# A two-layer diffusion backbone in one kernel: hand-overs at norms, first mixer projections and down products, and decay matrices built by accumulated products

## The chip, the cores and the metric

The kernel runs on one core of one Trainium2 chip. The metric is the device time of one execution in microseconds (us); lower is better. Each kernel is run several times and the median is given.

## What is computed

384 tokens (128 of context, 256 of latent, with weights in common) go through two layers of width 1024. Each layer is a SwiGLU feed-forward, a token mixer and a second feed-forward, each followed by a residual sum and a layer norm:

```python
def _layernorm(x, g, b):
    mu = mean(x); var = mean((x - mu)**2)
    return (x - mu) * rsqrt(var + LN_EPS) * g + b

def _layer(x, mod, p, states):      # sh, sc, g: nine parts of mod
    x = _layernorm(ALPHA * x + 0.5 * g1 * _swiglu(x * (1 + sc1) + sh1, w_gu[0], w_down[0]), ...)
    y, new_states = _token_mixer(x * (1 + sc2) + sh2, p, states)
    x = _layernorm(ALPHA * x + g2 * y, ...)
    x = _layernorm(ALPHA * x + 0.5 * g3 * _swiglu(x * (1 + sc3) + sh3, w_gu[1], w_down[1]), ...)
```

The mixer projects its input once (`w_in`) into the operands of three branches that run over the tokens forward and backward: HGRN2 (a gated linear recurrence), mLSTM (four heads with a matrix memory) and SSD (eight heads). The branches are projected, gated, summed and projected again (`w_out`). For mLSTM and SSD each head and direction needs a matrix of decays between tokens t and s of one block, which is masked to one triangle before the exponential:

```python
dlog = where(causal, b[t] - b[s] + i[s], -inf)          # mLSTM
s    = exp(dlog - m[t]) * (q @ k.T)
seg  = where(causal, a[t] - a[s], -inf)                 # SSD
y    = (exp(seg) * (C @ B.T)) @ (x * dt)
```

All is float32 in and out; the feed-forwards have 2816 hidden columns.

## The kernel before

**Layout and products.** Features lie on partitions in `KC` = 8 chunks of 128, the `T` = 384 tokens are columns. The weights are streamed once, in units of 512 KB (128 rows of 1024 columns), by SyncE's queue into four buffers `raw`. ScalarE rounds each unit to the fp32r type (`whi`, round_unit, L974), GpSimd subtracts to get the rest (`wlo`, L519, two halves a unit). TensorE then makes three products for each chunk instead of one in full fp32: high weight with high input, high with low input, low with high input (block_product, L552 to L554). Inputs are split in the same way: ScalarE shifts and scales a chunk (shifted, L1022, two pieces a chunk: context and latent tokens apart), rounds it to `h_hi` (rounded, L1028), and VectorE subtracts to `h_lo` (low, L1460). At the head of each projection three blocks are interleaved chunk by chunk (leading_products, L566 to L568), since the input's chunks come one after the other.

**What sets the order.** There is no scheduler: each engine's program is written out by hand, and counting semaphores order the engines. Some stages are separated by a meeting of TensorE, ScalarE and VectorE:

```python
def meet(eng, n):
    eng.drain().then_inc(met, 1)
    eng.wait_ge(met, 3 * n)
```

**The stages of a layer** and where they lie in layer 0 of the profiled execution: first feed-forward, gate and up products (122 to 307 us), its down products (309 to 404.7), norm (to 417.2), input projections (to 507), HGRN2 (to 654), rows of decays (to 741), mLSTM (to 797), convolution and states, SSD (939.5 to 1048), branches, output projection (to 1171.3), norm (to 1184.9), second feed-forward (to 1467.5), norm (to 1479.6). Layer 1 follows in the same way and ends with a norm that has no product behind it.

**Norms.** residual (VectorE, L1479) adds a block's output to `x`, one block of 128 features after the other. statistics (VectorE, L1482 on) subtracts an old mean, adds chunks 0 to 6 up in `sx` and their squares (ScalarE, squares, L1030) in `sqs` (L1512). layer_norm on TensorE (L595 to L604) makes four fp32 products with a matrix of 1/1024, two for the mean into bank 5 and two for the squares into bank 6: the sum of chunks 0 to 6, and chunk 7 by itself (L602 for the mean's second one). layer_norm on VectorE (L1515 on) then subtracts the mean from each chunk (L1527), forms the variance (L1533), takes the reciprocal of ScalarE's root (L1045; L1538), multiplies each chunk (L1543), and between those makes the low parts of the next input. Four subtractions stand ahead of the reciprocal.

**Banks of the input projections.** The plan (mixer_order, and L402 on) gives each projected block a bank of PSUM. `hf`, `hi` and `hg` are outputs of the input projection for HGRN2; `hf` comes first:

```python
kind, banks = "tm", (2, 3, 4) if name == "hi" else (5, 6, 7)
pool = {"rows": (3, 4), "ml": (3, 3), "pairs": (3, 7)}.get(stage, (0, 1))
banks = (b if name == "hf" and b < LEAD else pool[k % 2],)
```

So three leading blocks use banks 0 to 2, and the fourth bank 1 again, which ScalarE must have read out before (project_out and the bodies at L1303).

**Feed-forward.** Gate and up blocks go to banks 0 to 3; VectorE multiplies them (`vb`, L1563), copies to `act_hi` and subtracts to `act_lo`. Behind them all three engines go through ffn_met (L461): a meeting, and in the first feed-forward of layer 1 a reset of all counters instead. Then the down products start in banks 0 and 1.

**Decay matrices.** rows (VectorE, L1721 on) leaves in `x_5` one row of 384 numbers for each head and direction. For each of 8 rounds of mLSTM and 16 of SSD in a layer: spread (TensorE, L773) puts one row on all partitions by a fp32 product with a column of the identity, broadcast; exps (VectorE, L1808) adds the mask `neg` (-1e30 outside of the triangle) into `pt`; pair (ScalarE, L1217) takes the exponential with a per-row bias, three pieces of 128 columns; scores (VectorE, L1818 and L1823) multiplies with the products of q and k; TensorE's next products take that (L787 second product of a round, L805 heads, L810 to L812 and `carry`, L1837 on, for the carried state `cs`; L880 in SSD). L780 makes q with k. Between the rounds stand other projections of the same layer, by mixer_order.

## Time and profile before

| what | us |
|---|---|
| median of 3 runs (lowest to highest) | 2798.45 (2794.81 to 2804.83) |
| profiled execution: time / span in the trace | 2796.18 / 2794.3 |
| TensorE matmul, busy | 2431.0 |
| GpSimd, busy | 1518.8 |
| VectorE, busy | 1196.1 |
| ScalarE, busy | 1061.3 |
| ScalarE's rounding of a unit (L974), mean of one | 1.036 |
| GpSimd's rest of half a unit (L519), mean of one | 1.335 |
| VectorE's wait for ScalarE ahead of lastw (L1793, in rows), layer 0 and 1 | 11.58 and 10.37 |
| VectorE's wait for TensorE at the start (L1430) | 2.98 |

A line of the trace's timeline gives start and length in us, engine, line, operation, output and inputs by the program's names (without their buffer numbers), the shape, the count of like instructions in a row, and in brackets how long the engine had waited and for which instruction. A source view gives the number of instructions, the shortest, median and longest in ns, and the first and last start. The granted clock is given as a share: 1.00 is 2.4 GHz, 0.50 is 1.2 GHz.

### The profile page before, as it was taken

To read this page: it belongs to the slowest core of one execution; us is meant where nothing else is said; L and a number is where in the kernel's file an instruction comes from. 1 tells how busy PE (TensorE), PEld (TensorE's weight loads), DVE (VectorE), ACT (ScalarE), POOL (GpSimd) and SP (SyncE) were. 2 spreads that over 40 slices of the span, in tenths; PEclk is the share of its full clock that TensorE was granted. 3 is DMA by queue.
4 is the path that set the end of the run, shared out by engine and by line. 5 is a ranking of instruction groups with operands and counts; after the bars stand their busy time and mean duration, and the time that the engine had idled before them with its cause. 6 is when DMAs were issued, how large, how long until landed. Compare 5 with 4: busy or idle time off the path is not lost. (4 is left out here: it accounts for less than half of the span.)

```text
span 2794.3 us, 38271 instructions
## 1 busy us (share of the span) xinstructions
PE 2431.0 (87%) x13246; PEld 2222.2 (80%) x13246; DVE 1196.1 (43%) x1923; ACT 1061.3 (38%) x1631; POOL 1518.8 (54%) x1164
## 2 busy tenths in 40 slices
PE   5599989898878887799998999889987787889997
PEld 2499989787646676699998999788775676889997
DVE  4543232562565326643225331526445543663314
ACT  4333235434444443343234322452444324143322
POOL 3376545565555774466664655456743432646653
PEclk8799999999989998999999999999998888899999
DMA  8443333344343552234343333333432221324432
GB/s 277 144 141 122 118 108 109 103 129 129 102 128 94 159 158 83 83 120 123 118 128 100 124 112 118 97 113 121 144 105 83 85 66 61 98 76 135 128 111 70
DMA packets 93459, 323.16 MB, mean 116 GB/s; under 512 B 11040, under 2 KB 14368, under 8 KB 92960
## 3 DMA queue, kind: packets, MB, share of 16 engines
q1 hardware_dynamic: 87552, 312.03, 35.8%
q10 hardware_dynamic: 5792, 9.56, 1.0%
q8 instruction: 76, 1.25, 0.2%
q14 instruction: 39, 0.32, 0.0%
HBM read 317.35 MB, written 4.20 MB: 115 GB/s over the span
## 5 line engine op out<-in xcount | busy, mean ns | idle before, releaser
L519 POOL TENSOR_TENSOR wlo<-raw,whi 128x512 fp32r<-128x512 f32 (+2 forms) x1160 | 1518.6, 1335 | 1243.2 <-ACT whi L974 1182.0
L974 ACT CAST whi<-raw 128x1024 fp32r<-128x1024 f32 (+1 forms) x600 | 615.8, 1036 | 998.8 <-PE ps L554 666.4
L552 PE MATMUL ps<-h_hi,whi 128*128 128x384 f32 x2224 | 762.9, 343 | 35.2 <-DVE h_lo L2025 13.0
L554 PE MATMUL ps<-h_hi,wlo 128*128 128x384 f32 x2224 | 752.8, 339 | 0.0
L553 PE MATMUL ps<-h_lo,whi 128*128 128x384 f32 x2224 | 752.7, 338 | 0.0
L552 PEld LDWEIGHTS ps<-h_hi,whi 128*128 128x128 f32 x2224 | 425.5, 191 | 45.6 <-DVE h_lo L2025 13.6
L553 PEld LDWEIGHTS ps<-h_lo,whi 128*128 128x128 f32 x2224 | 425.4, 191 | 2.6 <-issue 2.0
L554 PEld LDWEIGHTS ps<-h_hi,wlo 128*128 128x128 f32 x2224 | 424.6, 191 | 0.0
L552 PE MATMUL ps<-act_hi,whi 128*128 128x384 f32 x704 | 241.9, 344 | 11.5 <-DVEq L458 5.9
L553 PE MATMUL ps<-act_lo,whi 128*128 128x384 f32 x704 | 240.4, 341 | 0.0
L554 PE MATMUL ps<-act_hi,wlo 128*128 128x384 f32 x704 | 240.3, 341 | 0.0
L1479 DVE SCALAR_TENSOR_TENSOR x<-ps,mod,x 128x128 f32<-128x128 f32 x96 | 35.6, 412 | 349.5 <-PE ps L554 349.5
L1560 DVE SCALAR_TENSOR_TENSOR sb<-tb,ps 128x384 f32<-128x384 f32 x88 | 48.8, 554 | 245.2 <-ACT tb L1061 245.2
L578 PE MATMUL ps<-whi,cond_s 128*4 128x512 f32 x288 | 123.7, 430 | 34.5 <-POOL wlo L519 34.5
L552 PEld LDWEIGHTS ps<-act_hi,whi 128*128 128x128 f32 x704 | 133.7, 190 | 13.3 <-DVEq L458 6.9
L1569 DVE TENSOR_TENSOR act_lo<-vb,act_hi 128x384 f32 x88 | 131.2, 1490 | 10.8
L553 PEld LDWEIGHTS ps<-act_lo,whi 128*128 128x128 f32 x704 | 133.5, 190 | 0.5
L554 PEld LDWEIGHTS ps<-act_hi,wlo 128*128 128x128 f32 x704 | 133.6, 190 | 0.0
L1563 DVE SCALAR_TENSOR_TENSOR vb<-sb,ps 128x384 f32<-128x384 f32 x88 | 48.8, 554 | 180.2 <-PE ps L554 180.0
L578 PE MATMUL ps<-wlo,cond_s 128*4 128x512 f32 x288 | 121.2, 421 | 0.0
L686 PE MATMUL ps<-q,kk 128*128 128x128 f32 x768 | 98.3, 288 | 22.8 <-DVEq L458 14.0
L686 PEld LDWEIGHTS ps<-q,kk 128*128 128x128 f32 x768 | 95.0, 202 | 28.0 <-DVEq L458 14.8
(311 smaller groups left out, 3011.7 us busy)
## 6 DMA issues: line engine op xcount, KB each, us to landing
raw<-in_w_in SPq DMA_DIRECT2D x248, 512.0 KB, 3.5
raw<-in_w_gu SPq DMA_DIRECT2D x176, 512.0 KB, 3.4
raw<-in_w_down SPq DMA_DIRECT2D x64, 512.0 KB, 3.4
raw<-in_w_mod SPq DMA_DIRECT2D x40, 512.0 KB, 4.5
raw<-in_w_down SPq DMA_DIRECT2D x32, 384.0 KB, 3.0
raw<-in_w_branch SPq DMA_DIRECT2D x24, 512.0 KB, 3.4
raw<-in_w_out SPq DMA_DIRECT2D x16, 512.0 KB, 3.4
x<-in_x ACTq DMA_DIRECT2D x1, 1536.0 KB, 6.9
```

Of the source, the lines that this page charges most:

```text
L519: last = nc.gpsimd.tensor_tensor(wlo[s][:, a:b], raw[s][:, a:b], whi[s][:, a:b].bitcast(F32), ALU.subtract)
L552: mm(out, hi_, xh[:, xc, :], start=start and n == 0, stop=False)
L553: mm(out, hi_, xl[:, xc, :], start=False, stop=False)
L554: last = mm(out, lo_, xh[:, xc, :], start=False, stop=stop and n == len(chunks) - 1)
L578: last = mm(bank[0:4, :], cond_s[:, 2 * m + c, :], w[s][:, c * MIX:(c + 1) * MIX], start=(m == 0 and c == 0 and w is whi), stop=(m == 3 an ...
L686: last = mm(out, kk[:, d, g, cols], (q if what == "diag" else qd[d])[:, g, cols], start=True, stop=True)
L974: act.copy(whi[m][:, 0:w], raw[m][:, 0:w]).then_inc(w_hi, 1)
L1479: last = stt(x[:, b, a:c], ps[b % 2][:, a:c], mod[:, col, gi:gi + 1], x[:, b, a:c], ALU.mult, ALU.add)
L1560: step(stt(sbf[jj][:, :], tb[jj][:, :], 1.0, ps[2 * jj][:, 0:T], ALU.add, ALU.mult))
L1563: stt(vb[jj][:, :], sbf[jj][:, :], 0.5, ps[2 * jj + 1][:, 0:T], ALU.mult, ALU.mult).then_inc(gated, 1)
L1569: step(tt(act_lo[:, bass.ds(f, 1), :], vb[jj][:, :].unsqueeze(1), act_hi[:, bass.ds(f, 1), :].bitcast(F32), ALU.subtract))
```

## The change

The change rewrites four kinds of places and touches what they share:

- *Norms.* Chunk 6 is no longer added to the sums: `sx` and `sqs` hold chunks 0 to 5 (`SUMMED` = 6), and chunks 6 and 7 each get a product of their own for mean and squares, six products instead of four. On VectorE two subtractions instead of four stand ahead of the reciprocal, and the low part of chunk n comes two steps behind its multiplication instead of three. On ScalarE chunk 0 is shifted and rounded before chunk 1 is shifted.
- *First mixer projections.* The blocks of that stage take banks 0 to 4 in turn; `hi` moves to banks 5 to 7 and `hg` to 2 to 4. ScalarE loads the tanh table ahead of the stage by a one-column activation.
- *Down products.* The meeting between gate and down products goes. TensorE waits for the count of gated chunks, and, within the first down block, for a new count of low parts (`ff_lo`), third by third. VectorE waits for that count, one step back, ahead of the product that overwrites `vb`. The reset of the counters in layer 1's first feed-forward stays (counts_reset).
- *Decay matrices.* spread makes three fp32r products accumulated in one bank: the identity with the mask, repeated for the three blocks of columns, and the broadcast column with the high and the low part of the rows (`x_5h`, `x_5l`, which rows splits on VectorE). VectorE's mask addition (exps) is gone, and the exponential reads PSUM. Identity and mask are rounded to fp32r once, at the start.

```diff
-        ident = sb("ident", [P, P])
+        ident_r = sb("ident_r", [P, P], F32R)
+        ident = ident_r[:, :].bitcast(F32)
...
-        neg = sb("neg", [P, 2, P])
+        neg = sb("neg", [P, 2, P], F32R)
...
+        (x_5h, x_5l, pr0, pr1, st0, st1), e3 = region(
+            rows0, ("x_5h", [P, T], F32R), ("x_5l", [P, T], F32R), *[(n, [P, T]) for n in ("pr0", "pr1", "st0", "st1")])
...
-        SHIFT_N = 3
+        SHIFT_N, SUMMED = 3, KC - 2
...
-                    kind, banks = "tm", (2, 3, 4) if name == "hi" else (5, 6, 7)
+                    kind, banks = "tm", (2, 3, 4) if name == "hg" else (5, 6, 7)
                 else:
                     kind = name if name in ("mod", "turn") else "fm"
-                    pool = {"rows": (3, 4), "ml": (3, 3), "pairs": (3, 7)}.get(stage, (0, 1))
-                    banks = (b if name == "hf" and b < LEAD else pool[k % 2],)
+                    pool = {"in": (0, 1, 2, 3, 4), "rows": (3, 4), "ml": (3, 3), "pairs": (3, 7)}.get(stage, (0, 1))
+                    banks = (pool[k % len(pool)],)
...
-        def ffn_met(eng, l, j, owner):
+        def counts_reset(eng, l, j, owner):
 
             if l == 0 or j == 1:
-                meet(eng, MEET["ffn", j])
...
-                pe.wait_ge(ln_y, j + 1)
-                mm(ps[5][:, 0:T], mean_w[:, :], sx[:, :], start=True, stop=False)
-                pe.wait_ge(ln_q, (KC - 1) * (j + 1))
-                mm(ps[6][:, 0:T], mean_w[:, :], sqs[:, :], start=True, stop=False)
-                pe.wait_ge(ln_cent, KC * (j + 1))
-                mm(ps[5][:, 0:T], mean_w[:, :], x[:, KC - 1, :], start=False, stop=True).then_inc(ln_mean, 1)
-                pe.wait_ge(ln_sq, KC * (j + 1))
-                mm(ps[6][:, 0:T], mean_w[:, :], sq[(KC - 1) % 4][:, :], start=False, stop=True).then_inc(ln_acc, 1)
+                for n in range(-1, 2):
+                    if n < 0:
+                        pe.wait_ge(ln_y, j + 1)
+                    else:
+                        pe.wait_ge(ln_cent, KC * j + KC - 1 + n)
+                    last = mm(ps[5][:, 0:T], mean_w[:, :], sx[:, :] if n < 0 else x[:, KC - 2 + n, :], start=(n < 0),
+                              stop=(n == 1))
+                    if n == 1:
+                        last.then_inc(ln_mean, 1)
+                    if n < 0:
+                        pe.wait_ge(ln_q, SUMMED * (j + 1))
+                    else:
+                        pe.wait_ge(ln_sq, KC * j + KC - 1 + n)
+                    last = mm(ps[6][:, 0:T], mean_w[:, :], sqs[:, :] if n < 0 else sq[(KC - 2 + n) % 4][:, :],
+                              start=(n < 0), stop=(n == 1))
+                last.then_inc(ln_acc, 1)
...
-                ffn_met(pe, l, j, "pe")
+                counts_reset(pe, l, j, "pe")
+                if l and not j:
+                    at = 0
+                pe.wait_ge(gated, at + NF + 2)
                 for b in range(KC):
                     pe.wait_ge(resid, 2 * KC * j + b + 1)
                     for third in range(KTHIRDS):
                         u = u0 + U_GU + KTHIRDS * b + third
                         unit_split(pe, l, u)
+                        if b == 0:
+                            pe.wait_ge(ff_lo, at + 2 + min(KC * (third + 1), NF))
...
-            def spread(r, rr):
-
+            def spread(r, d, rr):
+
+                out = ps[r % 2][:, 0:T]
                 if r >= 2:
-                    pe.wait_ge(pr_x, r - 1)
-                mm(ps[r % 2][:, 0:T], ident[:, rr:rr + 1].to_broadcast([P, P]), x_5[:, :], start=True,
-                   stop=True).then_inc(pr_bc, 1)
+                    pe.wait_ge(pr_e, r - 1)
+                mm(out.rearrange("p (a b) -> p a b", b=P), ident_r[:, :], neg[:, d:d + 1, :].to_broadcast([P, NT, P]),
+                   start=True, stop=False)
+                row = ident_r[:, rr:rr + 1].to_broadcast([P, P])
+                mm(out, row, x_5h[:, :], start=False, stop=False)
+                mm(out, row, x_5l[:, :], start=False, stop=True).then_inc(pr_bc, 1)
...
-                for n in range(KC + 1):
+                shifted(j + 1, 0)
+                rounded(j + 1, 0)
+                for n in range(1, KC + 1):
                     if n < KC:
                         shifted(j + 1, n)
-                    if n:
+                    if n > 1:
...
-                act.wait_ge(pr_x, r + 1)
+                act.wait_ge(pr_bc, r + 1)
...
-                    last = af(pr[r % 2][:, c], pt[r % 2][:, c], ACT.Exp, bias=t_1[:, t, rr:rr + 1])
+                    last = af(pr[r % 2][:, c], ps[r % 2][:, c], ACT.Exp, bias=t_1[:, t, rr:rr + 1])
...
+                af(eps[:, 2:3], eps[:, 0:1], ACT.Tanh)
...
+            cp(ident_r[:, :], ident_in[:, :])
+            cp(neg[:, :, :], neg_in[:, :, :])
...
-                    if n == 0:
+                    if n in (0, KC - 2):
                         continue
                     dve.wait_ge(ln_cent, KC * j + n + 1)
                     step.done()
                     sum_ = tt(sx[:, :], x[:, 0, :] if n == 1 else sx[:, :], x[:, n, :], ALU.add)
-                    sum_.then_inc(ln_y, 1) if n == KC - 2 else step(sum_)
-                for n in {4: (1,), 5: (2, 3), 6: (4, 5, 6)}.get(b, ()):
+                    sum_.then_inc(ln_y, 1) if n == KC - 3 else step(sum_)
+                for n in {4: (1,), 5: (2, 3), 6: (4, 5)}.get(b, ()):
...
-                shift(2)
-                shift(3)
                 dve.wait_ge(ln_std, j + 1)
                 step(nc.vector.reciprocal(rstd[:, :], std[:, :]))
                 step.done()
-                for n in range(KC + 3):
+
+                def normalised(n):
+
+                    dve.wait_ge(ln_sub, KC * j + n + 1)
+                    tt(x[:, n, :], x[:, n, :], rstd[:, :], ALU.mult).then_inc(ln_out, 1)
+
+                normalised(0)
+                normalised(1)
+                for n in range(2, KC + 2):
                     if n < KC:
-                        dve.wait_ge(ln_sub, KC * j + n + 1)
-                        tt(x[:, n, :], x[:, n, :], rstd[:, :], ALU.mult).then_inc(ln_out, 1)
-                    if n + 4 < KC:
-                        shift(n + 4)
-                    if not final and n >= 3:
-                        low(j + 1, n - 3)
+                        shift(n)
+                        normalised(n)
+                    if not final:
+                        low(j + 1, n - 2)
...
+                        dve.wait_ge(ff_lo, i * 2 + (at + jj + 1))
...
-                        step(tt(act_lo[:, bass.ds(f, 1), :], vb[jj][:, :].unsqueeze(1),
-                                act_hi[:, bass.ds(f, 1), :].bitcast(F32), ALU.subtract))
-                assert step.n - n0 == 6
-                step.off, step.n = 0, n0 + 6 * (U_GU // 4)
-                ffn_met(dve, l, j, "dve")
+                        tt(act_lo[:, bass.ds(f, 1), :], vb[jj][:, :].unsqueeze(1),
+                           act_hi[:, bass.ds(f, 1), :].bitcast(F32), ALU.subtract).then_inc(ff_lo, 1)
...
+                step(cp(x_5h[:, :], x_5[:, :]))
+                step.done()
+                step(tt(x_5l[:, :], x_5[:, :], x_5h[:, :].bitcast(F32), ALU.subtract))
...
-            def exps(r, d):
-                dve.wait_ge(pr_bc, r + 1)
-                if r >= 2:
-                    dve.wait_ge(pr_e, r - 1)
-                tt(pt[r % 2][:, :].rearrange("p (a b) -> p a b", b=P),
-                   neg[:, d:d + 1, :].to_broadcast([P, NT, P]),
-                   ps[r % 2][:, 0:T].rearrange("p (a b) -> p a b", b=P), ALU.add).then_inc(pr_x, 1)
```

VectorE at the end of the first norm (L1527 subtracts the mean, L1533 is the variance, L1543 multiplies, L1460 is the first low part), before:

```order
L1527 TENSOR_TENSOR x<-x,ps 128x384 [waits ln_dsq,ln_sq,ln_mean,dve_step]
L1533 TENSOR_TENSOR rstd<-ps,std 128x384 [waits ln_acc]
L1527 TENSOR_TENSOR x<-x,ps 128x384 [waits ln_sq] x3
L1538 RECIPROCAL rstd<-std 128x384 [waits ln_std]
L1543 TENSOR_TENSOR x<-x,rstd 128x384 [waits ln_sub,dve_step]
L1527 TENSOR_TENSOR x<-x,ps 128x384 [waits ln_sq]
L1543 TENSOR_TENSOR x<-x,rstd 128x384 [waits ln_sub]
L1527 TENSOR_TENSOR x<-x,ps 128x384 [waits ln_sq]
L1543 TENSOR_TENSOR x<-x,rstd 128x384 [waits ln_sub]
L1527 TENSOR_TENSOR x<-x,ps 128x384 [waits ln_sq]
L1543 TENSOR_TENSOR x<-x,rstd 128x384 [waits ln_sub]
L1527 TENSOR_TENSOR x<-x,ps 128x384 [waits ln_sq]
L1460 TENSOR_TENSOR h_lo<-ht_99,h_hi 128x384 [waits md_hi]
```

and of the change (L1550, L1556, L1559, L1565 and L1483 are the same operations in that order):

```order
L1550 TENSOR_TENSOR x<-x,ps 128x384 [waits ln_dsq,ln_sq,ln_mean,dve_step]
L1556 TENSOR_TENSOR rstd<-ps,std 128x384 [waits ln_acc]
L1550 TENSOR_TENSOR x<-x,ps 128x384 [waits ln_sq]
L1559 RECIPROCAL rstd<-std 128x384 [waits ln_std]
L1565 TENSOR_TENSOR x<-x,rstd 128x384 [waits ln_sub,dve_step]
L1565 TENSOR_TENSOR x<-x,rstd 128x384 [waits ln_sub]
L1550 TENSOR_TENSOR x<-x,ps 128x384 [waits ln_sq]
L1565 TENSOR_TENSOR x<-x,rstd 128x384 [waits ln_sub]
L1483 TENSOR_TENSOR h_lo<-ht_99,h_hi 128x384 [waits md_hi]
```

One subtraction instead of three now stands between variance and reciprocal, and three operations instead of seven between the first multiplication and the first low part.

TensorE from the last leading block to the fourth block of the input projections (the numbers are those of banks and tiles; `whi` and `wlo` are the weight's parts), before:

```order
L566 MATMUL ps2<-h_hi_62,whi2_55 128x384
L567 MATMUL ps2<-h_lo_63,whi2_55 128x384
L568 MATMUL ps2<-h_hi_62,wlo2_59 128x384
L552 MATMUL ps1<-h_hi_62,whi3_56 128x384 [waits w_split,evac]
L553 MATMUL ps1<-h_lo_63,whi3_56 128x384
L554 MATMUL ps1<-h_hi_62,wlo3_60 128x384
```

and of the change:

```order
L567 MATMUL ps2<-h_hi_62,whi2_55 128x384
L568 MATMUL ps2<-h_lo_63,whi2_55 128x384
L569 MATMUL ps2<-h_hi_62,wlo2_59 128x384
L553 MATMUL ps3<-h_hi_62,whi3_56 128x384 [waits w_split]
L554 MATMUL ps3<-h_lo_63,whi3_56 128x384
L555 MATMUL ps3<-h_hi_62,wlo3_60 128x384
```

The fourth block moved from bank 1 to bank 3, and its wait for the emptied bank (`evac`) is gone; the wait for the weights stays.

TensorE in the second round of mLSTM of layer 0 (`x_5` holds the rows, `ident` the identity, `cs` the carried state, `st` the scores; L585 is a projection's turn that stands between), before:

```order
L812 MATMUL ps7<-cs_162,mq_107 128x129
L585 MATMUL ps3<-pick_75,modrow_180 128x2 [waits evac]
L585 MATMUL ps3<-pick_75,modrow_180 128x2 x3
L773 MATMUL ps1<-x_5_135,ident_64 128x384 [waits pr_x]
L787 MATMUL ps7<-cs_162,mq_107 128x129 [waits ml_cu]
L805 MATMUL ps4<-va_109,st0_155 128x129 [waits ml_h,pr_s]
L805 MATMUL ps4<-va_109,st0_155 128x129 x2
L810 MATMUL ps6<-va_109,kw0_183 128x129 [waits ml_kw]
```

and of the change:

```order
L830 MATMUL ps7<-cs_164,mq_109 128x129
L586 MATMUL ps3<-pick_75,modrow_182 128x2 [waits evac]
L586 MATMUL ps3<-pick_75,modrow_182 128x2 x3
L788 MATMUL ps1<-neg_66,ident_r_64 128x384 [waits pr_e]
L791 MATMUL ps1<-x_5h_153,ident_r_64 128x384
L792 MATMUL ps1<-x_5l_154,ident_r_64 128x384
L805 MATMUL ps7<-cs_164,mq_109 128x129 [waits ml_cu]
L823 MATMUL ps4<-va_111,st0_157 128x129 [waits ml_h,pr_s]
L823 MATMUL ps4<-va_111,st0_157 128x129 x2
L828 MATMUL ps6<-va_111,kw0_185 128x129 [waits ml_kw]
```

Three products stand in the place of one, and they wait for ScalarE's exponential of two rounds before (`pr_e`) instead of VectorE's mask addition (`pr_x`).

## Rows read from the trace of the kernel before

**Rows 1.** The page, part 1: busy us, share of the span, instructions of each engine.

```profile
PE 2431.0 (87%) x13246; PEld 2222.2 (80%) x13246; DVE 1196.1 (43%) x1923; ACT 1061.3 (38%) x1631; POOL 1518.8 (54%) x1164
```

**Rows 2.** Stretches: window, us, busy PE, PEld, DVE, ACT, POOL, clock, DMA, GB/s.

```profile
140.00:210.00 70.00, 70.00 (x406) 70.00 (x405) 28.90 (x37) 21.02 (x25) 49.32 (x38) 1.00 0.45 143
310.45:313.80 3.35, 3.35 (x12) 3.35 (x12) 0.00 (x0) 0.00 (x0) 2.29 (x2) 0.50 0.00 0
...
1373.00:1376.50 3.50, 3.49 (x20) 3.49 (x21) 0.00 (x0) 1.04 (x1) 2.38 (x2) 1.00 0.01 5
```

**Rows 3.** Timeline of VectorE, end of the first norm.

```profile
408.83 1.47 DVE L1527 TENSOR_TENSOR x<-x,ps 128x384 f32<-128x384 f32 x3
410.22 2.54 DVE L1538 RECIPROCAL rstd<-std 128x384 f32<-128x384 f32 x1
412.80 0.56 DVE L1543 TENSOR_TENSOR x<-x,rstd 128x384 f32<-128x384 f32 x1
```

**Rows 4.** Timeline of TensorE, first norm and the first product behind it.

```profile
404.66 0.81 PE L598 MATMUL ps<-sx,mean_w 128*128 128x384 f32 x2
405.30 0.81 PE L600 MATMUL ps<-sqs,mean_w 128*128 128x384 f32 x2
406.25 0.91 PE L602 MATMUL ps<-x,mean_w 128*128 128x384 f32 x2
...
417.23 0.66 PE L566 MATMUL ps<-h_hi,whi 128*128 128x384 f32 x1 [9.42 <-DVE h_lo L1460]
```

**Rows 5.** Timeline of ScalarE, first norm: root, shifted chunks, rounding.

```profile
408.94 0.61 ACT L1045 ACTIVATE std<-rstd,eps 128x384 f32<-128x384 f32 x1 [1.26 <-DVE rstd L1533]
413.39 1.92 ACT L1022 ACTIVATE ht<-x,lnab 128x128 f32<-128x128 f32 x4 [3.83 <-DVE x L1543]
415.21 0.50 ACT L1028 CAST h_hi<-ht 128x384 fp32r<-128x384 f32 x1
```

**Rows 6.** Timeline, norm behind the output projection: VectorE, then TensorE.

```profile
1169.87 2.75 DVE L1512 TENSOR_TENSOR sqs<-sqs,sq 128x384 f32<-128x384 f32 x3
1172.54 0.73 DVE L1479 SCALAR_TENSOR_TENSOR x<-ps,mod,x 128x128 f32<-128x128 f32 x2
...
1177.89 2.54 DVE L1538 RECIPROCAL rstd<-std 128x384 f32<-128x384 f32 x1
...
1171.14 0.81 PE L598 MATMUL ps<-sx,mean_w 128*128 128x384 f32 x2
...
1173.92 0.91 PE L602 MATMUL ps<-x,mean_w 128*128 128x384 f32 x2 [0.33 <-DVE x L1497]
```

**Rows 7.** Timeline behind the leading blocks: ScalarE's table load, TensorE's fourth block.

```profile
432.14 1.28 ACT L1303 ACT_TABLE_LOAD   x1
...
435.69 0.44 PE L552 MATMUL ps<-h_hi,whi 128*128 128x384 f32 x1 [3.03 <-ACT kk L1303]
```

**Rows 8.** Timeline from the last gated chunk to the first down product.

```profile
307.26 0.55 DVE L1563 SCALAR_TENSOR_TENSOR vb<-sb,ps 128x384 f32<-128x384 f32 x1 [2.38 <-PE ps L554]
...
309.11 0.45 PE L552 MATMUL ps<-act_hi,whi 128*128 128x384 f32 x1 [1.98 <-DVEq L458]
```

**Rows 9.** Source views: mask addition, exponential from SBUF, an activation from PSUM.

```profile
L1808 DVE TENSOR_TENSOR pt<-neg,ps x48: 542/554/555, 742.0 to 2348.7; 128x384 f32<-128x384 f32 x48
...
L1217 ACT ACTIVATE pr<-pt,t x144: 384/387/405, 742.6 to 2349.9; 128x128 f32<-128x128 f32 x144
...
L1107 ACT ACTIVATE y_hg<-ps,par x24: 359/368/378, 683.7 to 2051.4; 128x128 f32<-128x128 f32 x24
```

**Rows 10.** Who waited for VectorE's carry and scores (us, times): mLSTM, last SSD.

```profile
  PE ps L787: 12.2, 11
...
  PE ps L805: 4.9, 8
  PE ps L780: 4.0, 6
...
  PE ps L880: 5.4, 5
```

**Rows 11.** Timeline of TensorE, an SSD round of layer 0 with its fourth unit.

```profile
971.72 0.40 PE L578 MATMUL ps<-whi,cond_s 128*4 128x512 f32 x1 [1.79 <-POOL wlo L519]
```

More of the change, by code:

```diff
@@ L788, in second @@
                        stop=True).then_inc(ml_i2, 1)
-                spread(0, 0)
+                spread(0, 0, 0)
                 head(0)
@@ L795, in mlstm @@
                     if r < 7:
-                        spread(r + 1, 32 * (1 - d) + (r + 1) // 2)
+                        spread(r + 1, 1 - d, 32 * (1 - d) + (r + 1) // 2)
                     if r:
@@ L868, in group @@
                     last.then_inc(pr_qk, 1)
-                spread(8, 64)
+                spread(8, 0, 64)
                 group(0)
@@ L1556, in ffn @@
                 with dve.Fori(0, U_GU // 4) as i:
-                    step.off = i * 6
+                    step.off = i * 4
                     for jj in range(2):
@@ L1791, in rows @@
                 dve.wait_ge(row_d, 3)
+                step.done()
+                step(cp(x_5h[:, :], x_5[:, :]))
+                step.done()
+                step(tt(x_5l[:, :], x_5[:, :], x_5h[:, :].bitcast(F32), ALU.subtract))
                 dve.wait_ge(row_a, 5)
@@ L2029, in _ @@
             for _ in range(2):
+                dve.sem_inc(ff_lo, 1)
                 dve.sem_inc(gated, 1)
```

56 lines of the change are left out of this document (26 added, 30 removed).

## The prediction, on record before the change was run

> **What bounds the kernel now.** I read the page's busy times first: TensorE is busy for 2431.0 of 2794.3 us [rows 1], so the time is its work plus its gaps, and an edit on another engine counts only where TensorE waits for it. Then the table by stretches [rows 2]: in a dense stretch 406 products of 128x384 take 70.00 us, 0.172 us each, at the granted clock 1.00 (2.4 GHz); behind some gaps the clock is 0.50 (1.2 GHz) and 12 products take 3.35 us, where after an equal gap with the clock kept 20 take 3.50 us. So a gap that is followed by such a stretch costs about 1.5 us more than its own length. Then I read the timelines at the four places that the diff touches, for what ends TensorE's wait there. The sum is made against the profiled execution, 2796.2 us (span 2794.3 and 1.9 around it); the median of the runs is 2.3 above that.
>
> **Norms.** TensorE stops with the last down product and starts again when the first low part of the next input is there: from 404.66 to 417.23 at the first norm [rows 4].
>
> *Later:* of chunks 6 and 7 now both go to the sums as products of their own. Before, two products (0.64 us apart, 404.66 and 405.30) stood ahead of the one that ends the mean, which started at 406.25. Now four stand there: 404.66 + 4 x 0.64 = 407.22, so mean, variance and root come 0.97 us later.
>
> *Earlier:* the reciprocal started at 410.22 [rows 3], though the root was ready at 408.94 + 0.61 = 409.55 [rows 5], because three subtractions (408.83, 1.47 us) stood ahead of it on VectorE. Now one does. It starts at 409.55 + 0.97 + 0.1 = 410.6, only 0.4 late.
>
> *Earlier again:* from the first multiplication (412.80 [rows 3]) to TensorE's start were 4.43 us, because ScalarE shifted two chunks (413.39, four pieces in 1.92 us) before it rounded the first (415.21 [rows 5]), and VectorE had seven operations between that multiplication and the first low part. Now: 0.59 to ScalarE's start, 0.96 for the two pieces of chunk 0, 0.50 rounding, 0.55 low part (VectorE, with three operations between, is there by then), 0.1 of hops: 2.7. That is 1.7 earlier; the net is 1.3 per norm, at three norms (the first of each layer, and the last of layer 0): -3.9. The later chunks come every 1.6 us (three VectorE operations each); TensorE needs 9 x 0.172 = 1.55 for one at full clock and twice that at its cold start, so it hardly waits for them.
>
> *The two norms behind the output projection* gain more. There VectorE is late: three additions of squares (1169.87, 2.75 us) keep the last residual until 1172.54, although TensorE ended at 1171.3 [rows 6]. With two additions it starts about 1171.5. The last mean product then starts at 1171.14 + 4 x 0.64 = 1173.7 instead of 1173.92, so the root is 0.2 earlier, and the reciprocal, freed of two subtractions, at 1177.1 instead of 1177.89: 0.8, plus the 1.7 of the hand-over: 2.5 each, -5.0.
>
> *The last norm* has no product behind it. It gets the 0.4, and two subtractions (0.47 each) now stand behind the reciprocal: +1.4. **Norms together -7.5**; bounds -2 (only the hand-over, at two norms) and -12 (no delay of the mean at all).
>
> **First mixer projections.** After the three leading blocks the fourth waited 3.03 us for ScalarE to empty bank 1, with a table load of 1.28 us in between [rows 7]. It now goes to bank 3 and the fifth to bank 4, both free: no wait. The next cover is the weights: the fifth block's unit can be rounded once the leading blocks end, about 1 us of emptying, 1.0 of rounding and 2 x 1.34 on GpSimd (the table of the profile) = 4.7 us after; TensorE has the rest of the leading blocks and 24 x 0.172, some 5.1 us, of work until then. So 3.0 goes, and the cold stretch that followed it in both layers, 1.5: 2 x 4.5, **-9.0**; bounds -5 and -9.5. The loading of the tanh table hides in ScalarE's idle time there. Ahead of the cover there is nothing else: the stage's end moves with TensorE.
>
> **Down products.** The last gated chunk ends at 307.26 + 0.55 = 307.8; TensorE starts at 309.11, after act_hi, act_lo and a meeting of three engines [rows 8]. Now it waits for the last gated chunk (banks 0 and 1 are read by then) and for the low parts of the first eight chunks only, long there: 307.9, 1.2 earlier. The low part of the last chunk is needed some 8 us later. This holds in three of four feed-forwards; in the third the counters are still reset in a meeting. In two of the three the gap was followed by a cold stretch [rows 2]; behind a gap of 0.8 us I take the clock as kept: -3 x 1.2 - 2 x 1.5, **-6.6**; bounds -3 and -6.6. The added wait on VectorE ahead of the gated product is for a subtraction one step back, done long before.
>
> **Decay matrices.** 48 times, a fp32 product (two passes) put a row on all partitions, VectorE added the mask (0.554 us, L1808), ScalarE took the exponential [rows 9]. Now three accumulated products do both. Their duration is not in the trace as such; the nearest row is the dense stretch, whose products have the same type, shape and a new weight block each: 3 x 0.172 = 0.52, against 0.64 for the two passes of a fp32 product (404.66 to 405.30 [rows 4]). Taken: 0.52. Upper bound: 0.45 each, half of the pair of passes at 406.25 that ran alone, 0.91 [rows 4]; 1.36 together. ScalarE's exponential reads PSUM instead of SBUF: 0.368 against 0.387 us on rows of 128 columns [rows 9], taken as no change.
>
> The Trainium skill, "VectorE: DVE Perf Modes", section on the TRN2 errata, gives ScalarE 172 fixed cycles from PSUM and 224 from SBUF, so by it three pieces would save 0.13 us a pair, an estimate of 2 to 3 us over the pairs on the path. The rows here show 0.02 a piece, so the sum stays without it.
>
> *mLSTM rounds* (16 in two layers): TensorE waits there for VectorE, 12.2 us for the carried state, 4.9 + 4.0 for the scores [rows 10]. The mask addition stood on VectorE ahead of the scores, and the exponential ahead of ScalarE's weighing of the second product, which the heads and the carried state wait for. Lower bound: one VectorE slot of 0.47 per round, 7.5. Upper bound: all those waits, 21, and 16 x 0.12 for the products. I take 10.5, because heads and carried state are late next on VectorE: what goes from the scores' waits comes back in part as a wait for the carried state. *SSD rounds* (32): 0.12 us each, 3.8. Where a round has no projection to fill it, the wait for scores of 5.4 in five places [rows 10] shrinks by the mask addition and its hops, 0.7: three such rounds and the two first ones, 3.5. In layer 0, four rounds wait 1.79 us for GpSimd's fourth unit [rows 11]; its rounding stands on ScalarE behind the exponential, which now starts 0.65 earlier: 2.6. **Decay together -20.4**; bounds -8 and -32.
>
> The two operations that split the rows (1 us, by L1808's size) fall into VectorE's wait of over 10 us for ScalarE in that stage; rounding identity and mask at the start falls into its wait of 3 us for TensorE (both waits in the table of the profile). Both at nothing; without that cover they would cost 2 x 1 us and 0.5 us.
>
> **Sum.** -7.5 - 9.0 - 6.6 - 20.4 = -43.5: 2752.7 for an execution like the profiled one, 2755.0 at the median's height. Forecast: **2754**.
>
> **Rivals.**
> 1. *The clock stretches come back elsewhere.* Gaps of 0.8 us remain at the down products, and one of three gaps of 2 us was not followed by a cold stretch, so length alone does not settle it. Without the 6 us of clock: 2760.
> 2. *GpSimd takes over.* It is busy for 54% of the span [rows 1] and makes TensorE wait in layer 0's SSD rounds already. If its splitting paces those rounds and the mLSTM rounds of layer 0, half the decay gain goes: 2764.
> 3. *The clock gains more.* Cold stretches lie in the mLSTM and SSD rounds too; six fewer at 1.5 are 9 us: 2745.
> 4. *The three products do not overlap.* At the upper bound of 0.45 us each, a row costs 0.71 more than now, 34 us, and the 5.7 I counted as saved go: 2795, no change.
> 5. *The other side, slower:* each product takes a whole isolated fp32 pair, 0.65 us, since one weight block is a single column spread out and the moving block a repeated mask. Then 48 x (1.95 - 0.65) = 62 stand against the other 43.5 - 5.7 = 37.8: 24.6 over the median, 2823. It decides from 0.48 us a product on, where 48 x (1.44 - 0.65) = 38 eats them. Against it: the fp32 row product used the same spread column, at no visible price.
>
> **How the numbers follow.** Chances: forecast 0.52, rival 1 0.13, rival 2 0.12, rival 3 0.16, rival 4 0.04, rival 5 0.03. The bounds of the terms move the forecast by some 15 up and down; the range 2738 to 2776 takes in rivals 1 to 3 and leaves out 4, 5 and the far ends of the bounds. 0.3% of 2798 is 8.4 us, about what a measurement can tell here. Faster by more: 0.93 (forecast, rivals 1 to 3); within: 0.04 (rival 4); slower: 0.03 (rival 5).
>
> **What would show it.** In the new trace: TensorE's gap at the first norm shorter by about 1.3 us with the reciprocal right behind the root; no gap behind the leading blocks; the down gap 0.8 us; three spread products within 0.55 us; no wait for a mask addition, a longer share of waits on the carried state. Wrong would be the forecast if a spread takes over 1 us, if GpSimd's waits grow by 10 us, or if cold stretches stand behind the shortened gaps.

## The result, and the profile after

The changed kernel takes **2762.37 us** (median of 4 runs, 2761.27 to 2765.39), beside 2796.63 for the kernel before on the same chip: a ratio of 0.9879, 95% interval 0.9862 to 0.9896. It is faster by 34.3 us. The forecast was 2754, a gain of some 43; the range of 2738 to 2776 holds the time.

The page's first part of the changed kernel; [rows 1] are those of before:

```profile
PE 2421.6 (88%) x13318; PEld 2228.6 (81%) x13318; DVE 1186.8 (43%) x1869; ACT 1057.6 (38%) x1633; POOL 1522.0 (55%) x1164
```

Busy times say little here: TensorE's fell by 9.4 us, the span by 33.9 (2794.3 to 2760.4). So most of the gain lies in gaps, and to find it I took the start of the first product of each stage from both timelines. The distance from one such start to the next, in us, both profiled executions:

| stage (layer 0 / layer 1) | before | after | difference | forecast |
|---|---|---|---|---|
| norms behind down products, a product follows (3) | 12.57, 12.58, 12.57 | 11.27, 11.27, 11.27 | -3.9 | -3.9 |
| norms behind the output projection (2) | 13.76, 13.75 | 11.27, 11.27 | -5.0 | -5.0 |
| last norm, to the end | 20.32 | 22.29 | +2.0 | +1.4 |
| input projections | 97.41 / 96.82 | 92.45 / 92.52 | -9.3 | -9.0 |
| gate and up, three feed-forwards | 187.19, 188.11 / 186.83 | 186.51, 186.58 / 186.34 | -2.7 | -3.6 |
| down products behind those | 95.55, 94.02 / 95.55 | 94.02, 94.02 / 94.02 | -3.1 | -3.0 |
| **gate and up, layer 1's first** | 192.77 | 198.29 | **+5.5** | 0 |
| mLSTM | 81.31 / 70.88 | 79.18 / 66.22 | -6.8 | -10.5 |
| SSD | 116.66 / 89.79 | 112.57 / 84.99 | -8.9 | -9.9 |
| HGRN2 | 219.54 / 215.85 | 215.73 / 219.16 | -0.5 | 0 |

What is left out comes to -1.3. Two lines differ from the forecast by clearly more than a microsecond: layer 1's first feed-forward, and mLSTM (SSD differs by 1.0).

The first norm in the new trace, TensorE, VectorE and ScalarE (lines as in [rows 3 to 5], shifted in the new file):

```profile
402.44 0.81 PE L603 MATMUL ps<-sx,mean_w 128*128 128x384 f32 x2
...
405.02 0.81 PE L603 MATMUL ps<-x,mean_w 128*128 128x384 f32 x2
...
413.71 0.66 PE L567 MATMUL ps<-h_hi,whi 128*128 128x384 f32 x1 [7.23 <-DVE h_lo L1483]
...
407.50 0.54 DVE L1550 TENSOR_TENSOR x<-x,ps 128x384 f32<-128x384 f32 x1
408.26 2.55 DVE L1559 RECIPROCAL rstd<-std 128x384 f32<-128x384 f32 x1 [0.22 <-ACT std L1063]
...
413.00 0.56 DVE L1483 TENSOR_TENSOR h_lo<-ht,h_hi 128x384 fp32r<-128x384 f32 x1
...
411.44 0.98 ACT L1040 ACTIVATE ht<-x,lnab 128x128 f32<-128x128 f32 x2 [3.21 <-DVE x L1565]
412.46 0.51 ACT L1046 CAST h_hi<-ht 128x384 fp32r<-128x384 f32 x1
```

The mean's last product starts 2.58 us behind the first (1.59 before), and now VectorE waits for ScalarE's root ahead of the reciprocal (0.22), where it was late before. The low part starts 4.74 us behind the reciprocal's start (408.26 to 413.00); before, TensorE got its first one 7.01 behind it (410.22 to 417.23), now 5.45.

The fourth block of the first input projections and the first down product; [rows 7 and 8] are those of before:

```profile
428.77 0.44 PE L553 MATMUL ps<-h_hi,whi 128*128 128x384 f32 x1 [0.69 <-POOL wlo L520]
...
308.42 0.44 PE L553 MATMUL ps<-act_hi,whi 128*128 128x384 f32 x1 [0.80 <-DVE vb L1591]
```

Gaps of 0.69 and 0.80 us are left of 3.03 and 1.98, and no cold stretch (products at the granted clock of about 0.5) follows. The 0.80 is what the forecast named; the 0.69, for GpSimd's part of the weights, was not foreseen at this block. In layer 1 the fourth block has no gap: its leading blocks end 15.25 us behind the stage's first product, those of layer 0 14.37.

The decay matrices, source views of the changed kernel (count, ns as shortest/median/longest, first and last start; the last line is of those that waited for the carried state):

```profile
L788 PE MATMUL ps<-neg,ident_r x48: 331/338/687, 729.4 to 2317.8; 128*128 128x384 f32 x48
L791 PE MATMUL ps<-x_5h,ident_r x48: 332/338/522, 729.7 to 2318.0; 128*128 128x384 f32 x48
L1237 ACT ACTIVATE pr<-ps,t x144: 342/368/370, 730.3 to 2319.1; 128x128 f32<-128x128 f32 x144
  PE ps L805: 20.1, 9
```

A product is shown with 338 ns, but the next one starts 0.17 us behind it in a dense stretch. One round of SSD in layer 0, TensorE:

```profile
964.52 0.34 PE L788 MATMUL ps<-neg,ident_r 128*128 128x384 f32 x1
964.69 0.34 PE L791 MATMUL ps<-x_5h,ident_r 128*128 128x384 f32 x1
964.87 0.33 PE L792 MATMUL ps<-x_5l,ident_r 128*128 128x384 f32 x1
```

The next product starts at 965.04, so the three take 0.52 us. The exponential takes 368 ns from PSUM, 387 from SBUF [rows 9]: 0.019 us a piece. The Trainium skill, "VectorE: DVE Perf Modes", section on the TRN2 errata, has 52 cycles between the two; the measured difference is less than half of the 0.043 a piece that the prediction's estimate took from it, and decides. TensorE's waits for the scores (4.9 and 4.0 [rows 10]) are gone, but the wait for the carried state is 20.1 us where it was 12.2 [rows 10].

### The profile page after: what moved, and what is told of

It is laid out like the page before. It is cut to its first block, busy times and chain, and to the rows that moved or that the text cites. A ratio compares the mean times of both kernels' runs of the same rounds, so it can differ in the third digit from the quotient of the medians.

```text
span 2760.4 us, 38398 instructions
## 1 busy us (share of the span) xinstructions
PE 2421.6 (88%) x13318; PEld 2228.6 (81%) x13318; DVE 1186.8 (43%) x1869; ACT 1057.6 (38%) x1633; POOL 1522.0 (55%) x1164
## 4 chain that ended last, share of the span: by engine, by line
issue 46%; POOL 42%; PE 10%; DVE 1%; POOLq 1%; ACT 0%; DVEq 0%; ACTq 0%
POOL wlo L520 42%; PE ps L553 3%; PE ps L555 3%; PE ps L554 3%; POOLq L534 0%; POOLq L532 0%; DVE ht L1476 0%; DVE x L1565 0%; DVE x L1550 0%; ACT whi L992 0%; DVE h_lo L1483 0%; DVE x L1577 0%; DVE rstd L1559 0%; PE ps L603 0%; PE ps L611 0%
## 5 line engine op out<-in xcount | busy, mean ns | idle before, releaser
L520 POOL TENSOR_TENSOR wlo<-raw,whi 128x512 fp32r<-128x512 f32 (+2 forms) x1160 | 1521.8, 1337 | 1204.1 <-ACT whi L992 1142.3
```

The costliest lines, as they stand in the source:

```text
L520: last = nc.gpsimd.tensor_tensor(wlo[s][:, a:b], raw[s][:, a:b], whi[s][:, a:b].bitcast(F32), ALU.subtract)
```

## The experiments

Twelve kernels, each run several times beside the kernel before. The changes are against the changed kernel unless the text says otherwise; "..." marks code left out. They were run in four sets, in which the kernel before had medians of 2793.4 to 2797.4 us. Only e2, e5, e6 and e12 have an interval of the ratio that stands clear of the changed kernel's (0.9862 to 0.9896); for the others the stages of the traces carry the reading, and the difference of the medians does not by itself. The stretch ahead of the first gate product, which no edit here touches, took 119.9 to 124.7 us in these traces.

**e1, an earlier wait at the layer boundary.** Layer 1's first feed-forward lost 5.5 us. Before it, ScalarE waits for VectorE's last affine operation of the norm, loads parameters, and only then rounds the weights of the fourth block.

```diff
-                    act.wait_ge(ln_x, KC * 4)
+                    act.wait_ge(ln_out, KC * 3)
```

> The changed kernel with one wait moved: at the layer boundary ScalarE waits for the last multiplication of the norm (24 counts of ln_out) instead of VectorE's last affine operation (32 counts of ln_x) before it loads the next parameters and rounds weights. Theory 1 (the hand-over of the norms made TensorE come early for a weight unit that ScalarE rounds only behind that wait, 4.48 us in layer 1's first feed-forward where 1.29 were before, with a cold stretch behind it): that wait falls under 0.6 us and the cold stretch goes, 4 to 6.5 us faster than the changed kernel, 2756 to 2758.5. Theory 2 (the missing 8 us are clock stretches and GpSimd's pace all over the program): the unit is late anyway, 2761 to 2763.

Measured: 2756.43 us (ratio to before 0.9854, 0.9832 to 0.9877), 6 faster than the changed kernel. ScalarE's way to the first rounding and TensorE's fourth block, timelines of the kernel before, of the changed one, and of e1:

```profile
1490.94 1.28 ACT L974 ACT_TABLE_LOAD   x1 [4.42 <-DVE x L1550]
...
1495.94 0.45 PE L552 MATMUL ps<-h_hi,whi 128*128 128x384 f32 x1 [1.29 <-POOL wlo L519]
```

```profile
1471.99 1.28 ACT L992 ACT_TABLE_LOAD   x1 [4.42 <-DVE x L1577]
...
1476.97 0.69 PE L553 MATMUL ps<-h_hi,whi 128*128 128x384 f32 x1 [4.48 <-POOL wlo L520]
```

```profile
1468.04 1.28 ACT L992 ACT_TABLE_LOAD   x1
...
1473.19 0.44 PE L553 MATMUL ps<-h_hi,whi 128*128 128x384 f32 x1 [0.26 <-POOL wlo L520]
```

The first product of that stage starts at 1479.61 before and at 1458.06 after; ScalarE's table load stands 11.3 us behind it before and 13.9 after. So VectorE's norm ends 2.6 us later, seen from TensorE. VectorE's last affine operations, before and after:

```profile
1487.09 3.21 DVE L1550 TENSOR_SCALAR x<-x,lnal 128x384 f32<-128x384 f32 x8
```

```profile
1468.14 3.21 DVE L1577 TENSOR_SCALAR x<-x,lnal 128x384 f32<-128x384 f32 x8
```

Counted from the norm's first product on TensorE (1467.03 and 1446.79), they end 23.3 us behind it before and 24.6 after, while TensorE's next stage starts 12.57 and 11.27 behind it. So half of the 2.6 us is TensorE's earlier start; the other half is that the change made VectorE itself end later: its reciprocal starts 0.26 us later behind the norm's first product, and from that to the end are 1.04 us more, in an order in which two more subtractions (0.47 each) stand there. With the wait moved the stage takes 191.66 us instead of 198.29: 4.2 of gap, and the stretch at a granted clock of 0.52 that followed it (17 products in 5.43 us). The other stages are as in the changed kernel to 0.7 us, but for two that are 2.2 and 2.5 longer (the one behind mLSTM in layer 1, and HGRN2 in layer 0), which the edit doesn't touch. Theory 1 holds.

**e2, the decay matrices as before.** spread, exps, pair and the split of the rows are those of the kernel before:

```diff
-                mm(out.rearrange("p (a b) -> p a b", b=P), ident_r[:, :], neg[:, d:d + 1, :].to_broadcast([P, NT, P]),
-                   start=True, stop=False)
-                mm(out, row, x_5h[:, :], start=False, stop=False)
-                mm(out, row, x_5l[:, :], start=False, stop=True).then_inc(pr_bc, 1)
+                mm(ps[r % 2][:, 0:T], ident[:, rr:rr + 1].to_broadcast([P, P]), x_5[:, :], start=True,
+                   stop=True).then_inc(pr_bc, 1)
...
+                    exps(r + 1, (r + 1) % 2)
...
```

> The changed kernel with the decay matrices as before (fp32 row product, mask added on VectorE, exponential from SBUF, no split of the rows). Theory 1 (the differences at the stages' ends in the two traces: mLSTM 7.4, SSD 9.0): 16.4 slower than the changed kernel, 2779. Theory 2 (the forecast's term of 20.4 holds, and the shortfall lies elsewhere): 2783. If the products cost what they save: 2763.

Measured: 2777.92 us (2776.87 to 2787.78), 15.6 slower. mLSTM takes 83.40 and 73.17 us, SSD 116.63 and 86.01. Theory 1 holds for the sum. Single stages differ from the kernel before with the same code: mLSTM is 2.1 and 2.3 us longer, at a mean granted clock of 0.84 and 0.84 instead of 0.90 and 0.88, and layer 1's SSD 3.8 shorter, at 0.98 instead of 0.92.

**e3, the norms as before** (sums, products, VectorE's and ScalarE's order):

```diff
-        SHIFT_N, SUMMED = 3, KC - 2
+        SHIFT_N, SUMMED = 3, KC - 1
...
                 shift(1)
+                shift(2)
+                shift(3)
                 dve.wait_ge(ln_std, j + 1)
...
```

> The changed kernel with the norms as before (chunk 6 in the sums, four products, VectorE's and ScalarE's old order). Theory 1 (6.9 gained at the norms themselves, of which 4.9 are lost again to the wait for ScalarE's rounding in layer 1's first feed-forward): 2 slower than the changed kernel, 2764.5. Theory 2 (the norms' term of 7.5 is kept): 2770.

Measured: 2766.29 us, 3.9 slower. The stages are back at 12.58, 13.76 and 20.34, and layer 1's first feed-forward at 192.93. So of the norms' 6.9 us, 5.4 were lost again in that one stage, because of the wait of e1, and 1.5 were left; the medians say 3.9.

**e4, the meetings back** in three of four feed-forwards:

```diff
...
             if l == 0 or j == 1:
+                meet(eng, MEET["ffn", j])
                 return
```

> The changed kernel with the meeting of the three engines put back between gate and down products in three of four feed-forwards (the counts stay). Both theories: 1.2 us each and 1.5 for a cold stretch behind two of them, 6 slower, 2768 to 2769. If the clock stays up behind the longer gap: 3.6 slower, 2766. If the counts and not the meeting were what mattered: 2762.

Measured: 2770.68 us, 8.3 slower. A meeting lengthens gate and up products by 1.3 (186.58 to 187.86) and 1.4 us (186.34 to 187.76), and behind one of three the down stage takes 95.55 instead of 94.02. With the first feed-forward (187.30 for 186.51) that is 5.0; the rest isn't in stages that the edit touches.

**e5, the banks as before**, and no early load of the tanh table:

```diff
-                    pool = {"in": (0, 1, 2, 3, 4), "rows": (3, 4), "ml": (3, 3), "pairs": (3, 7)}.get(stage, (0, 1))
-                    banks = (pool[k % len(pool)],)
+                    pool = {"rows": (3, 4), "ml": (3, 3), "pairs": (3, 7)}.get(stage, (0, 1))
+                    banks = (b if name == "hf" and b < LEAD else pool[k % len(pool)],)
...
-                af(eps[:, 2:3], eps[:, 0:1], ACT.Tanh)
```

> The changed kernel with the banks of the input projections as before (three leading banks, then 0 and 1 in turn) and no early loading of the tanh table. Theory 1 (the traces: 5.0 in layer 0 and 4.3 in layer 1): 9.3 slower than the changed kernel, 2771.7. If the gap behind the leading blocks is paid without a cold stretch: 6 slower, 2768. If the weights are late there anyway: 2762 to 2764.

Measured: 2777.08 us (2772.58 to 2780.23), 14.7 slower, more than any theory gave. The input projections take 95.76 and 97.44 us, 8.2 more than in the changed kernel. The profiled execution is 10.4 slower, and 2.6 of that lie ahead of the first gate product. The other 4 us of the median are not in that execution, and stay open.

**e6, three more mask products** for each decay matrix:

```diff
-                mm(out.rearrange("p (a b) -> p a b", b=P), ident_r[:, :], neg[:, d:d + 1, :].to_broadcast([P, NT, P]),
-                   start=True, stop=False)
+                for n in range(4):
+                    mm(out.rearrange("p (a b) -> p a b", b=P), ident_r[:, :],
+                       neg[:, d:d + 1, :].to_broadcast([P, NT, P]), start=(n == 0), stop=False)
```

> The changed kernel with the mask product of each decay matrix issued four times instead of once (144 products more in all; the mask is added four times). Each at 0.172 us, as the three products now follow one another, and none of it hidden: 24.8 slower, 2787. If the rounds of mLSTM hide theirs (48 of the 144) beside the wait for the carried state on VectorE: 16.5 slower, 2779. If a product costs the 0.45 of the upper bound: 65 slower, 2827.

Measured: 2781.33 us, 19.0 slower, nearest to the second case. By stages: mLSTM 79.14 and 68.21 (0.0 and +2.0), SSD 117.33 and 93.06 (+4.8 and +8.1). The SSD stage is counted from behind the first round's products, so in layer 1 these are 45 products in 8.07 us, 0.18 each. From the first of a round's products to the next product behind them the median round of SSD takes 1.045 us with six and 0.525 with three: 0.173 a product, the price that the prediction took. In layer 0's SSD part of them hides beside TensorE's waits for GpSimd's parts of the weights (8.0 us in the changed kernel, 6.2 here); in mLSTM most of it hides.

**e7, the carried state ahead of a head's scalings** on VectorE:

```diff
                     weights(r)
+                    if r >= 2:
+                        scaled(r - 2)
                     if r:
                         heads(r - 1)
                     carry(r)
```

(scaled holds the three operations L1892 or L1894 that ended heads; the count ml_h comes before them.)

> The changed kernel with VectorE's order in a round of mLSTM changed: the three scalings that end a head move behind the next round's scores and weights, so the carried state no longer waits for them, and the count that frees the head's bank comes before them. Theory 1 (what the mask addition left is now a wait for the carried state, 20.1 us in nine places, behind 24 us of scalings in 16 rounds): 6 to 14 faster than the changed kernel, 2748 to 2756. Theory 2 (VectorE's whole work in a round sets its length, so that the order does not matter): 2761 to 2764.

Measured: 2758.28 us (2754.90 to 2765.57), 4.1 faster by the medians: less than expected. mLSTM takes 73.34 us in layer 0 (5.8 less) and 68.88 in layer 1 (2.7 more), there with waits of TensorE like those of the changed kernel (7.5 against 8.8 us for the carried state) and a lower clock (mean 0.78 against 0.85).

**e8**, e1 and e7 together, with the old order in the last norm (shift(2) and shift(3) ahead of the reciprocal if final).

> Three edits on the changed kernel: the earlier wait for the parameters (e1), the later scalings in mLSTM (e7), and in the last norm all four subtractions ahead of the reciprocal again. Theory 1: 6 of e1, 6 to 14 of e7 and 1.4 to 2 of the last norm: 2740 to 2749. If e7 gives nothing: 2754 to 2755. If the last norm gives nothing, 2 more in either case.

Measured: 2752.43 us (2752.00 to 2765.53), above the expected span. The execution profiled took 2761.11. In it the last norm gave 0.6 (21.73), not 1.4 to 2, and mLSTM took 76.44 and 68.86 us: of e7's gain in layer 0 2.7 are there, and layer 1's loss is.

**e9, the carried state ahead of the whole head**, against e7:

```diff
-                    if r:
-                        heads(r - 1)
-                    carry(r)
+                    carry(r)
+                    if r:
+                        heads(r - 1)
```

> The kernel of e7 with the carried state updated ahead of the head's operations on VectorE instead of behind them (they wait for ScalarE, which waits for the product with the carried state of the round before, so that one late round made the next late). Theory 1 (that ring kept e7's gain down to 5.8 us in layer 0 and turned it into a loss of 2.7 in layer 1): TensorE's waits for the carried state, 14.9 us in e7, fall under 4, and the stage from mLSTM's first decay matrix to its end is 70 to 74 us in layer 0 and 60 to 65 in layer 1; 2745 to 2754 in all. Theory 2 (VectorE's work and GpSimd's hold on it set the round's length): 73 and 67 to 69, 2756 to 2759.

Measured: 2769.77 us, 11.5 slower than e7; 6.5 of that is in mLSTM, which takes 79.32 and 69.40 us. Waits in layer 0's mLSTM (for whom, total us, times, longest), TensorE's in e7, then TensorE's and VectorE's in e9:

```profile
PE ps L805 <- DVE cs L1880: 7.4, 4, 2.7
```

```profile
PE ps L823 <- DVE st L1842: 7.1, 3, 2.5
...
DVE co L1878 <- PE ps L830: 10.3, 6, 3.8
```

The wait for the carried state went, as expected, but TensorE now waits as long for the scores, which stand behind the head, and VectorE for TensorE. The kernel is slower than both theories allowed. e9 put one ring of waits in the place of another, so it does not show what sets the length of e7's rounds.

**e10, chunk 6 back in the sums**, the new order kept:

```diff
-        SHIFT_N, SUMMED = 3, KC - 2
+        SHIFT_N, SUMMED = 3, KC - 1
...
```

> The changed kernel with chunk 6 back in the sums (four products instead of six), all else of the norms as changed. By the forecast's terms the two products more cost 0.97 us at each norm and spare 0.8 at the two behind the output projection. Theory 1: norm to next product 11.27 becomes 10.3 behind the down products, the two of 11.26 behind the output projection 11.5 to 12.0, the last norm 22.29 becomes 21.3; layer 1's first feed-forward waits 1 us longer for its weights, so 2 slower to 2 faster in all, 2761 to 2764. Theory 2 (VectorE is late for the sums everywhere): all norms slower, 2765 to 2768.

Measured: 2760.12 us; the medians do not tell it from the changed kernel (2.3 less). The norms behind down products take 10.37 us (0.9 less), those behind the output projection 11.57 (0.3 more), the last 21.40 (0.9 less). So the two extra products pay only behind the output projection, and there little.

**e11 and e12, what follows from these.** e11 is e1 with chunk 6 in the sums behind down products only and the old order in the last norm; e12 adds e7.

```diff
-        SHIFT_N, SUMMED = 3, KC - 2
+        SHIFT_N, SUMMED, QUEUED = 3, (KC - 1, KC - 2, KC - 1), (0, 7, 13, 20)
...
```

> The changed kernel with the earlier wait of e1, chunk 6 in the sums for the norms behind the down products and apart for those behind the output projection, and all four subtractions ahead of the reciprocal in the last norm. By the measured stages: 6.6 of e1, 0.9 at each of the three norms behind down products that a product follows (2.7), 0.9 and 0.5 at the last: 10.7 faster than the changed kernel, 2751.7; cold stretches can move it by 2.5 to either side. If the gains at the norms are swallowed again by weights that come late (as in layer 1's first feed-forward before e1): 2755 to 2756.

Measured: 2755.98 us (2752.58 to 2762.31). The stages came as expected (10.37, 10.38, 10.38, 20.82 and 191.65), but the runs spread over 10 us, and the median doesn't tell it from e1.

> The kernel of e11 with e7's order in the rounds of mLSTM as well. If e7's gain in layer 0 (5.8 us) and its loss in layer 1 (2.7) both come back: 3.1 faster than e11, 2748.6. If the order sets nothing and both were cold stretches: no difference to e11 beyond 2.5.

Measured: **2743.68 us** (2740.18 to 2754.82; ratio to before 0.9833, 0.9817 to 0.9849): faster than both kernels. mLSTM takes 73.28 and 65.85 us: layer 0's gain of e7 came back, the loss in layer 1 did not. With the same order in those rounds TensorE's 263 products of layer 1's stage keep it busy for 50.4 us here, at a mean clock of 0.87, and for 55.3 in e7, at 0.78; the waits for the carried state are not shorter here (8.7 us against 7.5). So that loss was a matter of the clock.

## Why the prediction was right, and where it was off

*Norms.* Right by each place: 1.3 behind down products, 2.5 behind the output projection. e10 bears out the term of 0.97 for two more products (0.9 measured). Behind the output projection the lighter sums pay that price and 0.3 more. The last norm lost 2.0 instead of 1.4: its reciprocal came 0.26 us later (0.4 forecast), but from there to the end are 1.7 more, not the 0.9 of two subtractions. With these two ahead of the reciprocal again (e8, e11) 0.5 of it is left, and that stays open.

*The step that failed* is the sentence that the later chunks come every 1.6 us, so that TensorE hardly waits for them. It is true of the chunks, but it stopped there: it did not ask what stands behind the last chunk on VectorE, and who waits for that. ScalarE did, at the layer boundary, ahead of rounding weights, and 5.5 us were lost at one place; e1 shows it by itself. The forecast had half of the cause in hand: a later reciprocal and two subtractions behind it are its +1.4 of the last norm, but it counted that delay of VectorE's end at the last norm alone. A wait for GpSimd of 1.29 us stood at that place in the trace of before already.

*First projections.* -9.3 for -9.0: 5.4 of gaps (6.0 forecast) and 3.2 of cold stretches (3.0). The other 0.6 is chance: behind the norm, products follow one another by 0.32 us instead of 0.17 for a while, 18 of them before and 11 after in layer 0, 14 and 18 in layer 1. The cover named next, GpSimd's weights, was named for the fifth block, and 0.69 us of it showed at the fourth, in layer 0.

*Down products.* The gap went from 1.98 to 0.80, and both cold stretches went: 3 x 1.18 + 2 x 1.53 = 6.6, as forecast. The stages give 5.8, since the gate and up products also start cold behind their gaps: 13, 19 and 10 such products before, 16, 17 and 13 after.

*Decay matrices.* The price of 0.52 us for three products was right (e6: 0.173 each), which settles rivals 4 and 5. The sum of 20.4 measured 15.7 against the kernel before, and 16.3 against e2, both by stages. Its split is less sure. Against the kernel before, SSD gave 8.9 of 9.9 and mLSTM 6.8 of 10.5, less than its lower bound of 7.5; against e2, whose decay code is that of before, SSD gave 5.1 and mLSTM 11.2. So that SSD's term came out is in part luck of the clock. What holds in both is the wait: in mLSTM the prediction let the scores' waits come back "in part" as a wait for the carried state. 8.9 us went there, and 7.9 came back (from e2: 7.9 went, 8.4 came back).

*Rivals.* The cold stretches of rival 1 and 3 both happened, at places that the change does not touch, and cancelled: HGRN2 gained 3.8 in layer 0 and lost 3.3 in layer 1. Two stretches there, the same 24 products (with the first ones behind them) after a wait of 2.4 us, layer 0 and layer 1, in the kernel before:

```profile
547.36:553.00 5.64, 5.64 (x26) 5.60 (x27) 1.22 (x3) 0.00 (x0) 4.03 (x4) 0.52 0.54 146
1909.67:1913.00 3.33, 3.33 (x27) 3.24 (x28) 1.46 (x3) 0.00 (x0) 3.33 (x4) 1.00 0.34 100
```

and in the changed one:

```profile
538.51:541.50 2.99, 2.98 (x25) 2.95 (x26) 1.12 (x3) 0.00 (x0) 2.99 (x4) 1.00 0.38 107
1889.05:1894.60 5.55, 5.55 (x25) 5.55 (x26) 1.13 (x3) 0.00 (x0) 4.03 (x4) 0.50 0.51 155
```

The clock is 0.50 or 0.52 in one layer and 1.00 in the other, and they changed places. No edit decides it: in e10 HGRN2 takes 215.73 and 215.60 us, in e1 218.24 and 219.05, and neither touches it. That the two cancelled is luck. Rival 2 had its place in layer 0's SSD: TensorE's waits there for GpSimd's parts of the weights fell from 9.6 to 8.0 us, by 1.6 where the forecast counted on 2.6. In mLSTM they are 0.4 us; what GpSimd costs there by way of VectorE (last section) no run prices.

## What to carry to other kernels

When a stage is made to start sooner, list what its engines still do behind the hand-over and who waits for that: the first consumer gains, and a wait that was hidden behind the old start may come out, the more so where the edit moves work behind the hand-over. The start of the first product of every stage, in two traces side by side, shows such a loss in one row of a table, where totals by engine show nothing. Where waits of two microseconds can flip the clock, judge an edit by the stages it touches, not by the total of one run.

## What the runs showed of the hardware

Some of VectorE's small operations last nearly as long as GpSimd's (1.34 us) when both run. Timeline of VectorE in two rounds of mLSTM of layer 1, three scalings of 128x128 each:

```profile
2102.36 0.88 DVE L1894 SCALAR_TENSOR_TENSOR hout<-tmpb,den,hout 128x128 f32<-128x128 f32 x3
...
2111.56 3.69 DVE L1894 SCALAR_TENSOR_TENSOR hout<-tmpb,den,hout 128x128 f32<-128x128 f32 x3
...
2115.37 0.33 DVE L1870 SCALAR_TENSOR_TENSOR cs<-cs,wb,ps 128x129 f32<-128x129 f32 x1
```

and GpSimd's busy time in the stretches around them (the fifth "busy" of each row):

```profile
2102.30:2103.30 1.00, 1.00 (x6) 0.77 (x5) 0.96 (x5) 0.00 (x0) 0.00 (x0) 0.50 0.32 119
2111.50:2115.30 3.80, 3.80 (x18) 1.48 (x15) 3.76 (x5) 3.18 (x4) 3.80 (x4) 1.00 0.12 13
```

Without GpSimd three take 0.88 us, beside it 3.69. That fits with VectorE's busy time in the stage of mLSTM, 110 operations in either layer: 51.7 us in layer 0, where GpSimd is busy for 48.1, and 39.4 in layer 1, where it is for 28.1. The Trainium skill, "SBUF — State Buffer", section "SBUF: two separate sides", says that VectorE and GpSimd share a port pair as an exclusive lock, held for a whole instruction; VectorE takes it for an operation in a two-port mode, or for one with two SBUF inputs where GpSimd's operation reads SBUF. The trace agrees: L1894 has two SBUF inputs, and GpSimd's L520 reads its two from SBUF; the update of the carried state (L1870), with one input in PSUM, takes 332 to 343 ns in all of its 16 places, the one shown while GpSimd runs among them. No run here moved GpSimd's work out of these rounds; that is the next thing to try.
